# Two layers of a retention and differential-attention trunk: heads of the layers reordered, a state copied earlier, sample values on two column halves

## The reference, cut to what matters

```
h = rmsnorm(x); q_r,k_r,v_r,g_r, q_d,k_d,v_d, ga,gb = split(h @ w_in)
q_d = rope(rmsnorm(q_d)); k_d = rope(rmsnorm(k_d))      # 8 heads, 2 parts of 64
s = q_d . k_d (each part apart); p = softmax(s, visible chunks)
a = p[:, part 0] - lam * p[:, part 1]; o_d = a @ v_d
o_r, S = retention(q_r, k_r, v_r, S)                    # 4 heads, decayed, state S (128x256)
x += merge(o_r, o_d, gates) @ w_out;  x += conv_glu(rmsnorm(x))
```

## Time and the profile before

| | |
|---|---|
| time of three runs | 2244.57 us median (2242.88 to 2245.14) |
| the profiled execution | 2245.43 us, span 2243.5 us |
| TensorE busy / mean granted clock | 98% / 0.996 |
| VectorE, ScalarE, GpSimd busy | 54%, 44%, 38% |
| one D body (second of layer 0) | 74.04 us |
| the chain that ended last | TensorE 94%, ScalarE 2%, VectorE 1%, issue 1% |

### The profile page before, as it was taken

The page is one execution under the profiler, slowest core; times in us unless marked ns, Lnnn a source line. Parts: engine busy times, 40 slices in busy tenths (PEclk is TensorE's granted clock), DMA queues, the critical chain, the costliest instruction groups (busy, mean ns, idle before and its releaser), DMA issues.

```text
span 2243.5 us, 43652 instructions
## 1 busy us (share of the span) xinstructions
PE 2206.9 (98%) x17792; PEld 2097.3 (93%) x17792; DVE 1217.1 (54%) x2106; ACT 993.4 (44%) x1916; POOL 857.9 (38%) x378
## 2 busy tenths in 40 slices
PE   6999999999999999999999999999999999999998
PEld 6899889999999999999988889899899999999998
DVE  5676665555455553256255766565563556523553
ACT  4554554444323442344245555544452234424443
POOL 4244323334344443443443343232243434434433
PEclk9999999999999999999999999999999999999999
DMA  4232222221222222321322232222222222222222
GB/s 165 68 110 76 91 75 88 81 94 63 76 81 90 92 72 79 107 95 59 104 90 73 86 103 83 71 88 69 88 80 76 80 91 89 71 93 98 95 66 98
DMA packets 82231, 193.73 MB, mean 86 GB/s; under 512 B 7569, under 2 KB 36593, under 8 KB 82033
## 3 DMA queue, kind: packets, MB, share of 16 engines
q1 hardware_dynamic: 60272, 173.50, 23.6%
q10 hardware_dynamic: 21760, 17.45, 2.4%
HBM read 177.50 MB, written 13.42 MB: 85 GB/s over the span
## 4 chain that ended last, share of the span: by engine, by line
PE 94%; ACT 2%; DVE 1%; issue 1%; POOL 0%; DMA 0%; ACTq 0%; DVEq 0%; POOLq 0%
PE ps L627 14%; PE ps L629 14%; PE ps L628 14%; PE ps L678 7%; PE ps L679 6%; PE ps L680 6%; PE ps L1046 4%; PE ps L1045 4%; PE ps L1047 4%; PE ps L701 2%; PE ps L779 2%; PE ps L811 2%; PE ps L846 2%; PE ps L657 2%; PE ps L771 1%; PE ps L781 1%
## 5 line engine op out<-in xcount | busy, mean ns | idle before, releaser
L505 POOL TENSOR_TENSOR wlo<-raw,whi 128x1024 fp32r<-128x1024 f32 (+1 forms) x330 | 769.3, 2352 | 1061.6 <-ACT whi L1109 1061.6
L627 PE MATMUL ps<-hl,whi 128*128 128x272 f32 x2432 | 704.4, 290 | 0.0
L629 PE MATMUL ps<-hl,wlo 128*128 128x272 f32 x2432 | 701.9, 289 | 0.0
L628 PE MATMUL ps<-hl,whi 128*128 128x272 f32 x2432 | 700.5, 288 | 0.0
L627 PEld LDWEIGHTS ps<-hl,whi 128*128 128x128 f32 x2432 | 459.2, 189 | 1.5
L629 PEld LDWEIGHTS ps<-hl,wlo 128*128 128x128 f32 x2432 | 458.2, 188 | 0.0
L628 PEld LDWEIGHTS ps<-hl,whi 128*128 128x128 f32 x2432 | 457.7, 188 | 0.0
L1109 ACT ACTIVATE whi<-raw 128x1024 fp32r<-128x1024 f32 (+1 forms) x330 | 313.3, 997 | 202.9 <-PE ps L1047 176.5
L678 PE MATMUL ps<-whi,hl 128*128 128x256 f32 x1216 | 351.1, 289 | 5.6 <-ACT rawk L1204 4.4
L679 PE MATMUL ps<-wlo,hl 128*128 128x256 f32 x1216 | 344.8, 284 | 0.0
L680 PE MATMUL ps<-whi,hl 128*128 128x256 f32 x1216 | 344.3, 283 | 0.0
(11 more groups left out here) (237 smaller groups left out, 3377.5 us busy)
## 6 DMA issues: line engine op xcount, KB each, us to landing
raw<-in_w_units_dram SPq DMA_DIRECT2D x260, 512.0 KB, 4.7
raw<-in_w_down_units_dram SPq DMA_DIRECT2D x64, 352.0 KB, 3.4
out_new_k_prompt_dram<-rawk ACTq DMA_DIRECT2D x8, 512.0 KB, 3.0
out_new_v_prompt_dram<-vd ACTq DMA_DIRECT2D x8, 512.0 KB, 3.0
raw<-in_w_first_dram SPq DMA_DIRECT2D x6, 512.0 KB, 4.7
out_y_dram<-x SPq DMA_DIRECT2D x8, 272.0 KB, 6.3
kc_n<-in_cache_k_dram SPq DMA_DIRECT2D x8, 256.0 KB, 2.9
vc_n<-in_cache_v_dram SPq DMA_DIRECT2D x8, 256.0 KB, 3.3
```

Of the source, the lines that this page charges most:

```text
L505: e.tensor_tensor(wlo[:, s, a:b], raw[:, s, a:b], whi[:, s, a:b].bitcast(F32), ALU.subtract).then_inc(*S.up("w_ready", ("lo", j, part)))
L627: e.matmul(out, wh, hi, start=(c == 0), stop=False)
L628: e.matmul(out, wh, lo, start=False, stop=False)
L629: ins = e.matmul(out, wl, hi, start=False, stop=(c == KC - 1))
```

## The change

- Prologue: the low parts of the first unit are made by VectorE (`first_lo`), between its low parts of the activations, and no longer by GpSimd. The lambda products and sums come before VectorE's sums of squares.
- S: ScalarE takes the exponential of the lambdas before it waits for the norm; VectorE computes the lambda values before the sum of the query's sample rows.
- First D body of a layer: ScalarE copies key tile 0 and makes the high parts of the next weights before everything else; VectorE sums the key squares before it scales the queries, and GpSimd takes the key power before the low parts of the next but one unit; TensorE transposes the queries behind value tile 3 (before: 2). In every body the sums, means and reciprocals of the keys have places of their own (20 to 39).
- Sample steps: ScalarE copies all 64 columns of weights, VectorE adds none. TensorE multiplies with 64 columns, even blocks into rows 0 to 63 of bank o, odd blocks into rows 64 to 127. ScalarE copies rows 32 to 63 to `osum`; VectorE adds rows 64 to 95, 96 to 127 and 0 to 31 (`sum_of_sample`). For the first head of a body that stands behind combination 6; for the second in the next body behind the query sums, or at the start of R. TensorE waits for it before it writes bank o again.
- R: the copy of the state stands before the squares of the sample rows.

```diff
 # gpsimd
-            lo("P", 0)
...
                     if p == 0:
                         lo("D", 1)
                         power(20, "q", sem="qk_sum")
+                        power(20, "k", at=20, sem="qk_sum")
+                        lo("D", 2)
                     else:
...
-                    lo("D", 2, (0,))
-                    power(20, "k", sem="qk_sum")
-                    lo("D", 2, (1,))
+                        lo("D", 2, (0,))
+                        power(20, "k", at=20, sem="qk_sum")
+                        lo("D", 2, (1,))
 # tensor
-                    n_unit(0, hl1, banks=D_BANKS["k"])
+                    def sample_added(m):
+
+                        if D_BANKS["k"][m] == "o":
+                            e.wait_ge(*S.at("osum_done", "osum"))
+
+                    n_unit(0, hl1, before=sample_added, banks=D_BANKS["k"])
...
-                        if m == (2 if p == 0 else 1):
+                        if m == (3 if p == 0 else 1):
...
-                        acquire("o", act=1)
+                        acquire("o", act=1, dve=int(ib == NT))
+                        e.wait_ge(*S.at("act_free_t", ("aT", n)))
...
-                                ins = e.matmul(pv("o", DEC, HW), aTs[0:r, c, :], v, start=(c == 0), stop=(c == NT))
+                                rows = slice(2 * DEC * (c % 2), 2 * DEC * (c % 2 + 1))
+                                ins = e.matmul(ps[rows, BANK["o"]:BANK["o"] + HW], aTs[0:r, c, :], v, start=(c < 2), stop=(c >= NT - 1))
 # scalar
+                    e.wait_ge(*S.at("lam_ready", k=0))
+                    e.activation(lam_exp[:, :], lam_sum[:, :], ACT.Exp).then_inc(*S.up("act_step", key="lexp"))
                     e.wait_ge(*S.at("rs_ready", "rstd"))
...
+                    if p == 0:
+                        e.wait_ge(*S.at("kv_out", k=0))
+                        key_tile(0)
+                        hi("D", 1, 0)
+                        hi("D", 1, 1)
...
-                            e.activation(aTt[:, 0:NT, :], v[:, 0:NT, DEC:2 * DEC], ACT.Copy).then_inc(*S.up("act_free_t"))
+                            e.activation(aTs[:, 0:NT, :], v[:, 0:NT, :], ACT.Copy).then_inc(*S.up("act_free_t"))
...
+                            e.activation(osum, ps[DEC:2 * DEC, BANK["o"]:BANK["o"] + HW], ACT.Copy).then_inc(*S.up("act_free_o", key=("o", n)))
...
-                        squares(S, e, hh, NT)
                         e.wait_ge(*S.at("s_ready", ("sfin", hh)))
...
                         e.activation(sout[:, 0, :], pv("s0", P, RET_DV), ACT.Copy).then_inc(*S.up("act_free_s0", ("sfin", hh)))
+                        squares(S, e, hh, NT)
 # vector
+            def first_lo(part):
+
+                h = slice(part * UNIT // 2, (part + 1) * UNIT // 2)
+                e.wait_ge(*S.at("hi_ready", ("hi", 0, part)))
+                e.tensor_tensor(wlo[:, 0, h], raw[:, 0, h], whi[:, 0, h].bitcast(F32), ALU.subtract).then_inc(
+                    *S.up("w_ready", ("lo", 0, part)))
...
                 norm_lo(c, part, vecs[:, 0, c:c + 1])
+                if c in (1, 3):
+                    first_lo(c // 2)
...
+                def sum_of_sample(head, sem, key):
+
+                    for g in (2, 3, 0):
+                        e.wait_ge(*S.own())
+                        ins = e.tensor_tensor(osum if g else odif[0:DEC, NT, head * HW:(head + 1) * HW],
+                                              ps[g * DEC:(g + 1) * DEC, BANK["o"]:BANK["o"] + HW], osum, ALU.add)
+                        ins.then_inc(*(S.up("dve_step") if g else S.up(sem, key)))
...
                     def qk_sums(name):
+                        at = 20 if name == "k" else 0
...
+                        mean(20, DIFF_HD, name, at=at, sem="qk_sum")
...
                     qk_sums("q")
+                    if p:
+                        e.wait_ge(*S.at("act_free_o", k=0))
+                        sum_of_sample(2 * p - 1, "osum_done", "osum")
...
                     if p == 0:
-                        qk_apply(rawq, "q", 0, between=lambda: qk_sums("k"))
+                        qk_sums("k")
+                        qk_apply(rawq, "q", 0)
...
-                        e.tensor_tensor(aTs[:, 0:NT, :], v[:, 0:NT, 0:DEC], aTt[:, 0:NT, :], ALU.add).then_inc(
-                            *S.up("dve_free_t"))
...
                         combine(n)
+                        if n == NT + 2:
+                            e.wait_ge(*S.at("act_free_o", ("o", NT)))
+                            sum_of_sample(2 * p, "dve_free_o", "osum")
...
                 for _ in S.bodies("R"):
+                    e.wait_ge(*S.at("act_free_o", k=0))
+                    sum_of_sample(2 * 4 - 1, "osum_done", "osum")
```

More of the change, by code:

```diff
@@ L323, in program @@
             rinv = sb("rinv", [P, 4, 3], F32, s)
+        osum = rt[0:DEC, 0, 0:HW]
         with ExitStack() as s:
@@ L830, in weighted @@
                         else:
[L831 removed]
+                            acquire("t", act=2)
                             for c in range(TILES):
@@ L908, in outs @@
                             e.wait_ge(*S.at("dve_step", ("sT_lo", hh, ib)))
+                            if hh == 0 and ib == 1:
+                                e.wait_ge(*S.at("osum_done", "osum"))
                             if ib == 0:
@@ L1183, in square, with key_tile @@
                                          *S.up("act_step", key=("sq", name)))
+                    def key_tile(m):
+                        e.wait_ge(*S.at("mm_ready", ("N", 0, m)))
+                        e.activation(rawk[:, m, :], pv(D_BANKS["k"][m], P, UC), ACT.Copy, scale=rs1[:, m:m + 1]).then_inc(
+                            *S.up(f"act_free_{D_BANKS['k'][m]}", ("k", m)))
+                    if p == 0:
[3 more added lines that the diff above has]
+                        hi("D", 1, 1)
                     for s in ("dve_step", "dve_free_o", "kv_out", "o_ready", "t_ready", "dve_free_mm1", "dve_free_s1b",
@@ L1198, in act_program @@
                             bank = D_BANKS[name][m]
+                            if p == 0 and m == 0 and u == 0:
+                                continue
                             if m == 0 and u == 0:
@@ L1201, in act_program @@
                                 hi("D", 1, 1)
-                            if m < NT:
+                            if u == 0 and m < NT:
+                                key_tile(m)
+                            elif m < NT:
                                 e.wait_ge(*S.at("mm_ready", ("N", u, m)))
@@ L1294, in out @@
                         e.wait_ge(*S.own())
-                        dst = odif[0:r, ib, ds(p * 2 * HW + hh * HW, HW)]
-                        e.activation(dst, pv("o", r, HW), ACT.Copy, scale=rinv[0:r, n % 4, 0:1] if ib < NT else 1.0).then_inc(
-                            *S.up("act_free_o", key=("o", n)))
+                        if ib < NT:
+                            e.activation(odif[0:r, ib, ds(p * 2 * HW + hh * HW, HW)], pv("o", r, HW), ACT.Copy, scale=rinv[0:r, n % 4, 0:1]).then_inc(
+                                *S.up("act_free_o", key=("o", n)))
+                        else:
+                            e.activation(osum, ps[DEC:2 * DEC, BANK["o"]:BANK["o"] + HW], ACT.Copy).then_inc(*S.up("act_free_o", key=("o", n)))
                     take_filled(-1)
@@ L1672, in dve_program @@
                 norm_lo(c, part, vecs[:, 0, c:c + 1])
+                if c in (1, 3):
+                    first_lo(c // 2)
             normed_samples()
-            for c, part in CUT:
-                if c and part != 0:
-                    norm_sum(c, part)
             e.wait_ge(*S.at("lambdas", "in"))
@@ L1684, in dve_program @@
                 e.tensor_reduce(lam_sum[:, 2 * l:2 * l + 2], v[:, 0:2, :], AX, ALU.add).then_inc(*S.up("lam_ready"))
+            for c, part in CUT:
+                if c and part != 0:
+                    norm_sum(c, part)
             for l in S.layers():
@@ L1725, in qk_sums, with qk_apply @@
                     def qk_sums(name):
+                        at = 20 if name == "k" else 0
                         e.wait_ge(*S.at("act_step", ("sq", name)))
                         e.wait_ge(*S.own())
-                        e.tensor_reduce(ss[:, 0:20], prob[:, :, :].rearrange("p a b -> p (a b)")[:, 0:TILES * UC].rearrange(
+                        e.tensor_reduce(ss[:, at:at + 20], prob[:, :, :].rearrange("p a b -> p (a b)")[:, 0:TILES * UC].rearrange(
                             "p (g d) -> p g d", d=DIFF_HD), AX, ALU.add).then_inc(*S.up("qk_sum", key=("ss", name)))
-                        mean(20, DIFF_HD, name, sem="qk_sum")
-                    def qk_apply(buf, name, v, between=None):
+                        mean(20, DIFF_HD, name, at=at, sem="qk_sum")
+                    def qk_apply(buf, name, v):
                         e.wait_ge(*S.at("pool_step", ("rstd", name)))
```

38 lines of the change are left out of this document (12 added, 26 removed).

## The result

The changed kernel took 2228.09 us (median of four runs, 2227.85 to 2229.82) against 2244.86 (2242.88 to 2245.38) for the kernel before: ratio 0.9929, 95% interval 0.9911 to 0.9946. It is 16.8 us faster where 23.1 were forecast. The forecast of 2221.4 is 6.7 us too low; the range held the time. The profiled execution took 2227.85 us, span 2226.0, so 17.5 us less than that of before.

A forecast was written before the change was run, and what follows sets the result against it. TensorE, busy 98% of the span, was taken as the bound: only its idle time, slow-clock time and own work count. Terms 5.3 + 6.3 + 3.9 + 7.0 + 0.6 = 23.1 us gave 2221.4 us, range 2215.5 to 2230.

The forecast's parts named there:

- price of the new sum: VectorE's added sample sums: cost 0, without cover up to 1 us in each of 16 places; nothing in first bodies.
- TensorE waiting for the sum before key tile 2: Sign that the forecast is wrong: TensorE idles there, or before values 5, for VectorE's sum; no size given.
- the hole in the first body only moves: Rival: another low-half collision per layer, clock falls again; 2226.6 with one layer, 2231.8 with both; chance 0.18.
- First D body: First D body of each layer: shorter waits and no clock fall save 5.3 us in layer 0, 6.3 in layer 1.
- The leftover wait: Before the first bodies' query transposes, TensorE still waits 0.8 us in either layer, as low halves delay two rotations.
- R to M: Passage from R to M: two waits of 2.2 us together and a 1.7 us clock fall go; term 3.9.
- more is saved: Rival: no collision (+1.6), earlier start kept (+0.7), wait at 1581.1 gone; 2217.8 or less; chance 0.10.
- Sample values: Sample steps: two column halves overlap, saving 0.44 us in each of 16, 7.0 us in all.
- a gain near 0: Sample values by the skill page's row-group rule: loads stand in line, time about 2228; the prediction did not follow it.
- The sum itself: VectorE's sum takes 1.0 us: 2.6 to spare behind combination 6, next body's within 2.03 idle; cost 0.
- Prologue: First low weights on VectorE: TensorE starts at 12.85 instead of 14.13, but only 0.6 us is kept; bounds 0 and 1.3.

The follow-up runs named there:

- e1: Changed kernel with VectorE counting up osum_done at the head of the first D body instead of behind the query sums: 2218.75 us, ratio 0.9881.
- e7: Changed kernel with early mark and GpSimd's low half behind the query rotations (2216.70 us), but key tile 0 copied behind the query squares again: 2222.36 us.
- e5: Changed kernel with early mark (2218.75 us), but first bodies transpose the queries behind value tile 2 again: 2230.85 us, ratio 0.9932.
- e2: Changed kernel with all five blocks of a sample step on rows 0 to 63 of bank o: 2235.18 us, ratio 0.9954.
- e6: Changed kernel with early mark and GpSimd's low half behind the query rotations (2216.70 us), but first low halves on GpSimd again: 2221.35 us.
- e3: Changed kernel with the squares of the sample rows ahead of the copy of the state in R again: 2235.92 us, ratio 0.9953.

## Why the prediction was right, and where not

Where it failed is one sentence of the price of the new sum: "At the first body of a layer there is nothing to sum." That is true of the work and not of the wait. The diff shows that TensorE waits for `osum_done` in every body; in the first, the count comes from a mark, and the mark's place in VectorE's program is what I did not read. It stood behind the query sums, and these end 4.4 and 2.9 us after TensorE first wants key tile 2: priced at 0, the mark cost 4.4 + 1.7 + 2.9 = 9.0 us. e1, which moves nothing but the mark, shows it: 9.3 us. The text had named this sign ("TensorE waiting for the sum before key tile 2") without a price. The time also fell into the band of the rival "the hole in the first body only moves" (2226.6 with one layer, 2231.8 with both), but not by its mechanism: that was one more collision with a low half, which did not come. That the range held the time is partly luck too. The 9.0 us of the mark alone lead from 2221.4 to 2230.4, just past its end at 2230; gains that the sum had at nothing made up for it.

- *First D body.* Right in all parts that lie behind the mark. e7: the early key tile removes the wait. e5: the later transposes are worth their tile, with a clock fall that I had at 2.9 and 2.8 and that was 3.0. The leftover wait was forecast at 0.8 us by two caught rotations; the trace of after has two rotations of 2.40 and a wait of 0.76 and 0.77 over the usual spacing. By the Trainium skill's page "SBUF — State Buffer", section "Who interferes with whom", a VectorE instruction with two SBUF inputs and a GpSimd instruction that reads SBUF contend, and whoever has the shared ports holds them alone. The traces agree: beside a low half a rotation took 2.40 instead of 0.33, and a scaling 3.72 instead of 1.55.
- *R to M.* Right: 3.9 forecast, 3.8 measured (2.3 for the waits, 1.5 for the clock). Missing were the other effects of the same edit: 0.22 us at each passage between heads, and the wait at 1581.10, which the rival "more is saved" had. ScalarE's copy of the state now comes right behind the product (508.02 below), and the squares (L1627, 509.56) behind it:

```profile
508.02 0.38 ACT L1436 ACTIVATE sq<-ps 128x256 f32<-128x256 f32 x1 [0.48 <-PE ps L952]
509.56 0.37 ACT L1627 ACTIVATE sq<-ps 32x256 f32<-32x256 f32 x1 [1.16 <-DVE oret L1991]
```

- *Sample values.* Right by mechanism: 0.38 us a step against 0.44. The first eight records took 0.58 us to the ninth where they had 0.99, so the four pairs gained 0.41; the two records of block 4 start 0.36 us before the next work where they had 0.33, the small price of wider loads. The Trainium skill's page "TensorE: Matmul & The Clock Gate", section "Part 3: Packing small matmuls", has a weight load overlap a matmul only if its row group differs. The prediction worked out from it a gain near 0. It passed over the table of the same section, where three column tiles give 2.38 times. e2 decides against a gain near 0: the column halves are worth 0.43 us a step.
- *The sum itself.* Free, as said, where there is something to sum. In the second body it takes 0.9 us of VectorE's time that lay idle (the idle time before the scaling fell from 2.03 to 1.01), and behind combination 6 it is done at 170.8, 2.3 us before TensorE writes the bank again (173.07):

```profile
113.94 0.61 DVE L1760 TENSOR_TENSOR rt<-ps,rt 32x128 f32<-32x128 f32 x2
114.59 0.28 DVE L1760 TENSOR_TENSOR odif<-ps,rt 32x128 f32<-32x128 f32 x1
...
169.89 0.61 DVE L1760 TENSOR_TENSOR rt<-ps,rt 32x128 f32<-32x128 f32 x2 [1.05 <-ACT rt L1321]
170.53 0.28 DVE L1760 TENSOR_TENSOR odif<-ps,rt 32x128 f32<-32x128 f32 x1
```

- *Prologue.* 0.6 forecast. TensorE started 1.3 us earlier and was 1.2 ahead at the first key tile. There it waited for the next low halves, which came only 0.8 earlier, and 0.9 was left. But the reason was only half of it: I counted what VectorE takes over and not what it no longer loses to GpSimd (e6: 3.6 us). In before, the seven low parts took 9.04 us too.

Adding up: 23.1 forecast, less 9.0 for the mark, less 1.0 at the sample steps and 0.1 from R to M, plus 1.3, 1.1, 0.3 and 0.2 of which the sum knew nothing, is 15.9; the 1.6 that are left to 17.5 are the first bodies, which without the mark were better than forecast. 1.1 of it lie in layer 1: before waited 0.69, 0.12 and 0.35 us at 1188.34, 1191.58 and 1194.66, ahead of scores and gate, and after waits 0.18 at the last of them alone. In layer 0 the prologue kept 0.9 where 0.6 was forecast. Without the mark's mistake the forecast would have been 2.7 us too high (e1, 2218.75).

## What to carry to other kernels

When a change adds a wait, go through every iteration in which the waiter runs, the first one above all, and find the instruction or the bare mark that releases it there and what stands ahead of it in its program. A mark that stands for no work belongs ahead of everything that waits. And work that is moved off an engine must be costed for what it did to its neighbours: the low half of GpSimd cost VectorE more than taking the work over did.

## What the hardware showed that I had not expected

- The clock's fall behind a hole is not a matter of its length alone. The same hole of layer 1 (2.95 us over the usual spacing) was followed by a clock of 1.00 in after and in e2, and of 0.50 for 6.8 us in e3; a shorter one of 2.56 us in e7 was followed by 0.50 for 3.40. A hole of about 1.1 us before `spread` brought it down at 514.93 and in e3 twice, but not at 1626.39 of before; one of 1.09 us before the transposes (e1) and one of 0.76 before key tile 3 (e7) did not. The longest did each time: 3.22 and 3.19 us of before, 4.28 of after (4.3 in e2 and e3 as well), 3.71 and 3.39 of e5.
- One copy in another place (e3) was worth 7.6 us, of which 3.0 are the clock.
